# Choosing the PSUM bank of each product in a long interleaved stage by the turn of its last reader

## The reference

```
h = rms_norm(x, norm_mix_g[l])
proj = h @ w_in[l]
o_a = mla_branch(mla_cols, ...)            # softmax attention, 8 heads
o_b = rwkv7_branch(rw_cols, ...)           # fwd + bwd recurrence
x = x + (gates[:, :, 0] * y_a + gates[:, :, 1] * y_b) @ w_merge[l]
...
x = x + (silu(conv(h @ w_ffn_gate[l])) * (h @ w_ffn_up[l])) @ w_ffn_down[l]
```

## Time and profile before

| | us |
|---|---|
| median of 3 runs (3253.57 to 3256.72) | 3255.03 |
| the profiled execution, its own time | 3253.55 |
| its span from first to last instruction | 3251.3 |
| the stage of recurrences and attention | 531 to 1289 |

### The profile page before, as it was taken

The page is one execution under the profiler, slowest core; times in us unless marked ns, Lnnn a source line. Parts: engine busy times, 40 slices in busy tenths (PEclk is TensorE's granted clock), DMA queues, the critical chain, the costliest instruction groups (busy, mean ns, idle before and its releaser), DMA issues.

```text
span 3251.3 us, 62204 instructions
## 1 busy us (share of the span) xinstructions
PE 3132.6 (96%) x26688; PEld 2561.6 (79%) x26688; DVE 2084.1 (64%) x3018; ACT 1343.6 (41%) x2442; POOL 937.5 (29%) x810
## 2 busy tenths in 40 slices
PE   8999998999999988999999999999999999999998
PEld 8678776887788777787888888878677878888887
DVE  5263465666766665856999778752555575655686
ACT  4333334555555444533433344442332343333444
POOL 1232243222222142501576640000000025666100
PEclk9999999999999999999999999999999999999999
DMA  4241245112112122552222347422002312322753
GB/s 152 68 155 52 72 158 169 56 42 64 64 45 63 54 82 71 165 191 79 94 104 97 110 159 247 158 96 93 33 27 96 131 68 101 107 101 98 268 159 117
DMA packets 128018, 346.48 MB, mean 107 GB/s; under 512 B 15792, under 2 KB 19520, under 8 KB 124928
## 3 DMA queue, kind: packets, MB, share of 16 engines
q1 hardware_dynamic: 106592, 258.09, 23.8%
q0 software_dynamic: 21152, 84.42, 7.0%
HBM read 246.51 MB, written 95.94 MB: 105 GB/s over the span
## 4 chain that ended last, share of the span: by engine, by line
PE 84%; DVE 9%; ACT 4%; issue 2%; POOL 1%; DMA 1%; SPq 0%; DVEq 0%; ACTq 0%; POOLq 0%
PE ps L378 41%; PE ps L377 39%; PE ps L381 3%; DVE AR L387 2%; DVE X L387 2%; DVE SM L398 1%; DVE W L387 1%; ACT AR L384 1%; DVE WS L387 1%; DVE HT L391 0%; ACT WS L384 0%; ACT W L2379 0%; POOL AR L387 0%; ACT X L384 0%; DVE EX L387 0%
## 5 line engine op out<-in xcount | busy, mean ns | idle before, releaser
L387 DVE TENSOR_TENSOR WS<-W,WS 128x512 fp32r<-128x512 f32 (+1 forms) x284 | 341.7, 1204 | 245.8 <-ACT WS L384 245.6
L377 PE MATMUL ps<-HH,WS 128*128 128x512 f32 x1280 | 394.2, 389 | 0.0
L377 PE MATMUL ps<-TO,WS 128*128 128x512 f32 x1440 | 345.9, 389 | 0.0
L384 ACT ACTIVATE WS<-W 128x512 fp32r<-128x512 f32 (+1 forms) x284 | 210.0, 740 | 310.4 <-PE ps L378 165.2
L377 PEld LDWEIGHTS ps<-TO,WS 128*128 128x128 f32 x1440 | 270.3, 188 | 56.1
L377 PEld LDWEIGHTS ps<-HH,WS 128*128 128x128 f32 x1280 | 240.2, 188 | 49.9
L377 PE MATMUL ps<-HL,WS 128*128 128x512 f32 x640 | 249.0, 389 | 0.0
L378 PE MATMUL ps<-HH,WS 128*128 128x512 f32 (+1 forms) x736 | 230.3, 394 | 1.2 <-ACT HH L384 1.2
L377 PE MATMUL ps<-TO 128*128 128x512 f32 x936 | 226.8, 390 | 0.2 <-DVE TO L387 0.2
L378 PE MATMUL ps<-AR 64*64 64x64 f32 (+2 forms) x5440 | 202.8, 241 | 22.6 <-ACT AR L384 11.4
L384 ACT ACTIVATE X<-ps 128x512 f32<-128x512 f32 (+1 forms) x168 | 100.5, 598 | 284.5 <-PE ps L378 129.4
(11 more groups left out here) (387 smaller groups left out, 6530.5 us busy)
## 6 DMA issues: line engine op xcount, KB each, us to landing
AR_b<-h_d SPq DMA_DIRECT2D x154, 256.0 KB, 2.9
AR<-rw_d SPq DMA_DIRECT2D x104, 256.0 KB, 4.2
W<-in_w_fg SPq DMA_DIRECT2D x44, 512.0 KB, 3.8
W<-in_w_fu SPq DMA_DIRECT2D x44, 512.0 KB, 5.1
h_d<-FST POOLq DMA_DIRECT2D x20, 1024.0 KB, 4.4
x_d<-X POOLq DMA_DIRECT2D x24, 512.0 KB, 4.5
W<-in_w_tok SPq DMA_DIRECT2D x24, 512.0 KB, 4.0
rw_d<-X POOLq DMA_DIRECT2D x40, 256.0 KB, 3.3
```

The lines of the kernel that those rows point to most:

```text
L377: return pe.e.matmul(o, l, r, start=start, stop=stop, skip_group_check=True)
L384: return e.e.activation(o, x, ACT.Copy)
L387: return e.e.tensor_tensor(o, x, y, op)
```

## The change

The bank is no longer the next of the round in this stage. Both passes now do the choosing. In the counting pass it is the round as before; there, `sig` also records for each instruction the turn in which it stands on its engine (`turn_of`). In the second pass, for a take from MAIN inside the stage, `pick` goes over all places of the ring and takes the one with the lowest cost. `free_from` of a bank is the highest turn among the last readers of its user (0 if it has none). For a pair the cost is whether that turn is not yet over (here >= turn), then the turn itself. For a single bank that is free, a bank whose partner of the pair is not free comes first, then the lower turn of its readers. Among equals Python's `min` gives the lowest bank number. Since the second pass does not move the round's counter in the stage, MAIN's round starts elsewhere behind it.

```diff
+    def free_from(self, spot):
+        if spot not in self.user:
+            return 0
+        return max(self.turn_of[self.same.get(k, k)] for k in self.frees[self.user[spot]])
+
+    def pick(self, ring, n, turn):
+        def cost(at):
+            here = max(self.free_from(s) for s in ring[at:at + n])
+            if n > 1 or here >= turn:
+                return here >= turn, here, 0
+            other = self.free_from(ring[at ^ 1])
+            return False, other < turn, here
+        return min(range(0, len(ring), n), key=cost)
+
-    def next_place(self, ring, key, n=1):
-        if self.counting:
+    def next_place(self, ring, key, n=1, turn=0):
+        if not self.counting and ring == self.earliest and turn:
+            at = self.pick(ring, n, turn)
+        else:
             at = self.ring.get(ring, 0)
             at += (-at) % n
             self.ring[ring] = at + n
-            spots = [ring[(at + i) % len(ring)] for i in range(n)]
-            ...
+        spots = [ring[(at + i) % len(ring)] for i in range(n)]
+        self.place[key] = spots[0]
+        self.before[key] = [self.user[s] for s in spots if s in self.user]
+        for s in spots:
+            self.user[s] = key
...
     def sig(self, name, *key, frees=None):
         self.now = (name, key)
+        self.plan.turn_of[self.now] = self.turn
...
-            b = plan.next_place(banks, key, n)[1]
+            b = plan.next_place(banks, key, n, pe.turn)[1]
...
         MAIN, SIDE = BANKS[0:6], BANKS[6:8]
+        plan.earliest = MAIN
...
+        def counted(e):
+            for _ in range(400):
+                e.turn += 1
+                yield
...
             for _ in range(7):
+                e.turn += 1
                 next(s0)
                 next(mid)
                 next(at_)
-            interleave(s0, mid, s1, at_)
+            interleave(counted(e), s0, mid, s1, at_)
+            e.turn = 0
```

More of the change, by code:

```diff
@@ L71, in __init__ @@
         self.sems, self.value, self.frees, self.place, self.before, self.ends = {}, {}, {}, {}, {}, {}
-        self.same = {}
+        self.same, self.turn_of, self.earliest = {}, {}, None
     def begin(self, counting):
@@ L130, in __init__ @@
     def __init__(self, plan, e, name):
-        self.plan, self.e, self.name, self.seen, self.now = plan, e, name, {}, None
+        self.plan, self.e, self.name, self.seen, self.now, self.turn = plan, e, name, {}, None, 0
     def wait_ge(self, sem, value):
```

## The result

The median of four runs is **3317.8 us** (3315.02 to 3325.1) against 3254.3 (3251.52 to 3256.72) for the kernel before on the same chip: the ratio over all runs is 1.0198, with a 95% interval of 1.0186 to 1.0211 (that of the two medians is 1.0195). The change makes the kernel 63.5 us slower. The forecast was 3290, its range ended at 3316: direction and mechanism were right, the size was not. The profiled execution took 3315.02 us.

The account below looks back on a forecast made before the run. TensorE was taken to bound the kernel, busy 3132.6 of 3251.3 us. Late takes less offsets, 66.5 - 6.3 - 3 - 15 - 7.6 = 34.6 us, gave 3288.2, with 1.5 for the median 3290; range 3257 to 3316.

Parts of the forecast that it names:

- What bounds the kernel, and the placement: Whole kernel: TensorE busy 3132.6 of 3251.3 us; in the stage, 61 us idle of 758; 706 of 848 takes change bank.
- The order among equals: MAIN's stage takes: 428 of 848 have ties, lowest number wins; in 193 its reader was not the first to end.
- The 66.5 us of late takes: Stage: products late at 95 places because the new bank's reader ends later, 66.5 us in all; ACT's pT copies 26.7.
- the 6.3 of waits gone: Stage: old waits for banks that the new choice ends, in 33 places, 6.3 us taken off.
- The 78 waits on semaphores, 3 us: TensorE: semaphore waits fall from 1260 to 1182; 3 us taken off, of 0 to 3.
- The two terms of absorption, 15 + 7.6 us: Stage: 15 us present idle time inside new waits, only renamed; 7.6 us, half of 15, idle time behind them.
- U of 1132.68: Stage: product held till 1134.73 by D8's copy behind three exponentials; its successor waits 1.51 us for ACT anyway.
- turns 20 and 21: Stage, counted: M 3, Y, second pT and X4 delayed, V's wait gone; 3.1 us net.
- its own rival: Stage: DVE and ACT catch up while TensorE stands, so new waits are absorbed; 3246 at full effect, faster, chance 0.10.
- nothing absorbed: Upper end of the forecast's own range: no absorption behind or inside the waits, 66.5 - 9.3 = 57 us, so 3312.
- the clock falls too: Stage: new idle time brings 5 to 15 clock dips, 10 to 25 us on top of 34.6; 3300 to 3315, chance 0.15.
- Behind the stage: After the stage: MAIN's round starts one bank off, 0.6 us less and 0.6 us more waiting cancel; 1962 us as before.

Follow-up runs that it names:

- e4: Changed kernel with the fixed round inside the stage again, on a counter of its own; 3253.62 us, ratio 1.0 to the kernel before.
- e1: Changed kernel with ties of equal cost going to the bank taken longest ago, pair rule kept; 3262.96 us, ratio 1.0027 to the kernel before.
- e3: Changed kernel without the pair rule and with ties going to the bank taken longest ago; 3252.96 us, ratio 0.9999 to the kernel before.
- e7: Changed kernel with banks read by ACT for attention counted as read half a turn later; 3289.03 us, ratio 1.0107 to the kernel before.
- e5: Kernel before with MAIN's 848 stage takes from a table of banks made from measured reader end times, pair rule included; 3245.1 us, ratio 0.9977.
- e8: Kernel before with all 912 stage takes, over all eight banks, from a table made from measured reader end times; 3242.36 us, ratio 0.9962.
- e6: Kernel before, banks unchanged, with 64 added TensorE waits for ACT's copy of the second pT; 3309.47 us against 3253.62, ratio 1.0174.
- e9: Kernel before with the four transposes of each tile's second pT written three times, 512 more, no added wait; 3303.88 us against 3254.3, ratio 1.0155.

## Why the prediction was wrong in size

**What bounds the kernel, and the placement.** Right. The loss is idle time of TensorE in the stage, DVE's and ACT's busy time did not move (500.45 and 379.31 us against 499.82 and 380.10), and e4 shows that the choice alone does it.

**The order among equals.** Right, and the square of e1 to e3 weighs it: of 63.5 us, 51 to 55 hang on ties that go to the lowest number. The pair rule was in the count of 66.5 but had no name of its own in the prediction; it is 10 to 14 us.

**The 66.5 us of late takes and the 6.3 of waits gone.** Right: 60.2 net, against +63.2 in the trace. The terms hold by kind, too: e7 takes out attention's share and pays what is left. The rows that were to rise most did: ACT's copies from 13.5 to 15.1 + 11.7 + 4.7 + 4.6 = 36.1 us, DVE's L406 from 5.7 + 4.8 = 10.5 to 9.2 + 6.2 + 6.1 + 5.3 = 26.8. L400's waits for ACT are there, nine for W with 4.6 us; V's is gone. Idle time in the stage went to 111.5 us, not to some 95, and its end to 1349, not 1323.

**The 78 waits on semaphores, 3 us.** Not to be seen. Of the 78, only 23 were instructions of their own, by the page's total. e4 can't test the term, since its page has as many instructions as that of before. e5 and e8, with 44 and 47 fewer, gained 8.5 and 11.3 us where the count, which has no such term, said 9.0 and 14.1.

**The two terms of absorption, 15 + 7.6 us: this step failed.** Without them and the 3 us for semaphores its sum is 60.2, against 63.5 measured. The prediction took present idle time inside the new waits as "only renamed", and half of what lies behind them as made good. The waits for data fell by 2.6 us, not 22.6. The example on which it rested, U of 1132.68, was read rightly and behaved so (2.03 us of wait, 0.5 us of loss). What was wrong was to take it as the pattern for the whole list. As turns 20 and 21 show it, ACT or DVE needs what TensorE makes next: delay the product, and its copy comes later, and the wait for that copy is as long as it was, only shifted. e6 shows this by itself: 58.3 us of waits added, the other rows of the list down by 4.4, 55.9 paid. Old idle time absorbs a new wait only where the releaser of the old one does not hang on the delayed product; ACT's three exponentials ahead of D8's copy were such a case. That it is rare here is read from the sums; the other places were not gone through one by one. The prediction wrote this dependence down as a reason against its own rival ("products of the same group that need the delayed one") and then did not apply it to its own sum. Its end "nothing absorbed", 3312, was the nearest of its own values.

**The clock.** The rival "the clock falls too" was half right, and smaller than its 10 to 25 us. Its sign, a granted clock under 0.96 in the stage, did not come: it was 0.97, forecast 0.98. Stretches of the stage after:

```profile
700.00:800.00 100.00, 88.82 (x1874) 73.62 (x1876) 66.47 (x126) 50.67 (x111) 27.30 (x32) 1.00 0.19 59
```

```profile
1150.00:1200.00 50.00, 43.35 (x990) 36.61 (x986) 25.38 (x52) 17.65 (x39) 11.39 (x13) 0.86 0.37 129
1200.00:1250.00 50.00, 41.46 (x1181) 36.39 (x1175) 28.33 (x60) 20.16 (x43) 21.25 (x21) 0.93 0.12 40
1250.00:1300.00 50.00, 42.16 (x1165) 35.73 (x1162) 33.08 (x65) 18.37 (x40) 12.84 (x14) 0.97 0.04 14
1300.00:1349.00 49.00, 37.29 (x1055) 32.60 (x1051) 21.26 (x50) 16.55 (x37) 12.48 (x13) 0.87 0.24 83
```

The stage's end before, to set beside them with the last two lines of the earlier trace rows:

```profile
1100.00:1150.00 50.00, 46.13 (x1176) 38.97 (x1170) 31.00 (x63) 22.13 (x48) 11.40 (x14) 1.00 0.37 128
1150.00:1200.00 50.00, 44.01 (x1290) 38.38 (x1290) 30.60 (x65) 21.70 (x47) 21.48 (x21) 0.97 0.12 41
```

In 700 to 800 TensorE is idle for 11 us of 100, where it was for 6, and the clock is 1.00, where it was 0.98. The other hundreds from 600 to 1100 are alike: idle for 11 to 14 us of each, at a clock of 0.98 to 1.00, the same two values as before. The clock falls in the last quarter: the mean of its four stretches is near 0.91, where the four from 1100 on had some 0.95 before. That is about 20 of the 23 us more at 1.2 GHz (an estimate from these shares). Some 7 us go to the clock: in part it made up for the little that was absorbed, and it may be what moved the result past the range's end, by 1.8 us. The rival's price, 2 us for a stretch of 100 us at 0.98, is 0.5 us per us at 1.2 GHz; the books have about 0.3. The Trainium skill, TensorE: Matmul & The Clock Gate, section on psum-queue depth-cycling, tells of a kernel whose clock swung to and fro because TensorE idled briefly between groups of matmuls while it cycled through the banks. In e6 and e9 the trace agrees in direction (51.2 us at 1.2 GHz with waits, 27.3 with work), but here it is the smaller part of the loss by far: some 7 us of 67.

**Behind the stage.** Right: 1963.7 us against 1962.8; the shift of MAIN's round cancels, and e4, which shifts it too, is at 1.0.

**The rule on banks.** The prediction cited the Trainium skill, Perfetto Trace Analysis, section Matmuls, that independent groups should rotate through the banks. The runs agree: the round (e4) and the rule nearest to it (e3) cost nothing, and the kernels that leave it by turns, with ties to the lowest number, cost up to 2%. e5 and e8 add to it that the round is not the best order, but 0.2 to 0.4% from one that knows the readers' times.

**Left open:** how the 7 us over the count divide between the clock and the few us absorbed, since each is known only as a difference of single executions; and why the clock fell where it did, in the last quarter of the stage, and not in the middle.

## What to carry to other kernels

Where buffers are handed out by a planner, look at the ties first: a program step is too coarse a clock when 4.3 buffers are taken per step from six, and then the tie-break is the rule; break ties by age, or use times from a trace. Price each take by the end of its new releaser against its start, and subtract existing idle time behind it only if that idle time's own releaser does not depend on the delayed work; without that proof the loss is the whole sum. A gain from better placement is bounded by the waits for buffers that exist now, 18.3 us here, and a part of it can come back as waits for data.

## What of the hardware was unexpected

Some 57 us more of work in the stage (e9) left the time at 1.2 GHz about where it was, 27.3 us against 30.7, while 58 us more of waiting in the same places (e6) brought it from 30.7 to 51.2. Yet the waiting kernel's stage was only 6.4 us longer than the working one's (814.5 and 808.1). In the middle of the stage, 700 to 800, nearly double the idle time, 11 us in place of 6, cost no clock at all. And nothing was given back behind a wait in turns 20 and 21: 3.1 us of delay counted from the ends of the readers became 3.4.
